# Constant loads on other queues, and the last turns of three stages inside the next job's fourth granule

## The reference

```python
# layer 1: sparse attention (NSA) and gated delta rule (GDN), merged by gates, then an MLP
h = rms_norm(x, ln1_w)
proj = h @ w_in
o_a = nsa_attention(nsa_q, nsa_kv, nsa_gate, rel_table, pe_k, pe_v, w1_k, w2_k, w1_v, w2_v)
o_b = gated_deltanet(gdn_qkv, gdn_z, gdn_a, gdn_b, conv_w, a_log, dt_bias, gdn_norm_w)
x = x + (g_a * (o_a @ w_pa) + g_b * (o_b @ w_pb)) @ w_o
h = rms_norm(x, ln2_w)
x = rms_norm(x + square(relu(h @ w_up)) @ w_down, ln_f_w)
# layer 2: attention with a forget gate (FOX)
y = (softmax_attention(q, k, v, forget) * silu(gate)) @ fox_w_out      # q, k, v, gate = x @ fox_w_in
x = layer_norm(ALPHA * x + y)
# layer 3: retention (RET)
y = (group_norm(retention(q, k, v)) * silu(gate)) @ ret_w_out          # q, k, v, gate = x @ ret_w_in
x = layer_norm(ALPHA * x + y)
```

## Time and profile before

| | us |
|---|---|
| three runs | 3129.84, 3130.97, 3135.68 (median 3130.97) |
| the profiled execution, from its first instruction to its last | 3131.4 |
| PE busy in it | 2893.7 (92%) |
| DVE busy | 1660.0 (53%) |
| ACT busy | 1297.6 (41%) |
| POOL busy | 54.6 (2%) |
| mean granted TensorE clock | 0.970 of full |

### The profile page before, as it was taken

The page is one execution under the profiler, slowest core; times in us unless marked ns, Lnnn a source line. Parts: engine busy times, 40 slices in busy tenths (PEclk is TensorE's granted clock), DMA queues, the critical chain, the costliest instruction groups (busy, mean ns, idle before and its releaser), DMA issues.

```text
span 3131.4 us, 36002 instructions
## 1 busy us (share of the span) xinstructions
PE 2893.7 (92%) x13617; PEld 2396.2 (77%) x13617; DVE 1660.0 (53%) x1879; ACT 1297.6 (41%) x1558; POOL 54.6 (2%) x57
## 2 busy tenths in 40 slices
PE   4998988899998999999999799999989999999997
PEld 3877777687777888888888677777767777877776
DVE  3554654744454555555555555555565455554555
ACT  3554633523434444444344444444334443443432
POOL 0000000000000000000000000000000000000000
PEclk9999999999999999999999999999989999999998
DMA  5753322314565556565655468568545554554553
GB/s 189 199 202 111 126 85 77 110 66 146 176 215 188 167 188 191 186 197 181 198 185 191 123 145 153 149 144 160 201 140 164 169 164 161 189 174 154 172 188 135
DMA packets 258376, 505.71 MB, mean 161 GB/s; under 512 B 12920, under 2 KB 22216, under 8 KB 256848
## 3 DMA queue, kind: packets, MB, share of 16 engines
q1 hardware_dynamic: 249552, 489.72, 51.1%
q0 software_dynamic: 2864, 13.32, 1.6%
q10 hardware_dynamic: 5840, 0.94, 0.2%
HBM read 500.26 MB, written 3.67 MB: 161 GB/s over the span
## 4 chain that ended last, share of the span: by engine, by line
PE 60%; issue 33%; DVE 3%; DMA 1%; ACT 1%; ACTq 1%; POOL 1%; DVEq 0%; POOLq 0%
PE acc L295 18%; PE acc L296 18%; PE acc L297 18%; PE mx L336 1%; DMA bias_by_distance<-arena 1%; PE acc L1423 1%; PE acc L1424 1%; PE acc L1425 1%; ACTq L800 1%; ACT w_hi L259 1%; PE mx L1559 0%; PE mx L1547 0%; ACT arena L383 0%; DMA arena<-bias_by_distance 0%; POOL sm L403 0%
## 5 line engine op out<-in xcount | busy, mean ns | idle before, releaser
L267 DVE TENSOR_TENSOR w_lo<-raw,w_hi 128x1024 fp32r<-128x1024 f32 x924 | 1133.1, 1227 | 1292.7 <-ACT w_hi L259 1279.9
L259 ACT ACTIVATE w_hi<-raw 128x1024 fp32r<-128x1024 f32 x924 | 978.7, 1060 | 1571.3 <-PE acc L297 1505.6
L295 PE MATMUL acc<-w_hi,lt_a_hi 128*128 128x512 f32 x2592 | 1040.4, 401 | 3.0 <-DVE w_lo L267 3.0
L296 PE MATMUL acc<-w_lo,lt_a_hi 128*128 128x512 f32 x2592 | 1018.3, 393 | 0.0
L297 PE MATMUL acc<-w_hi,lt_a_lo 128*128 128x512 f32 x2592 | 1017.8, 393 | 0.0
L295 PEld LDWEIGHTS acc<-w_hi,lt_a_hi 128*128 128x128 f32 x2592 | 494.2, 191 | 107.7 <-issue 7.2
L297 PEld LDWEIGHTS acc<-w_hi,lt_a_lo 128*128 128x128 f32 x2592 | 492.0, 190 | 105.2
L296 PEld LDWEIGHTS acc<-w_lo,lt_a_hi 128*128 128x128 f32 x2592 | 493.5, 190 | 102.0 <-issue 3.8
L295 PE MATMUL acc<-w_hi,lt_b_hi 128*128 128x512 f32 x896 | 351.0, 392 | 0.0
L297 PE MATMUL acc<-w_hi,lt_b_lo 128*128 128x512 f32 x896 | 349.8, 390 | 0.0
L296 PE MATMUL acc<-w_lo,lt_b_hi 128*128 128x512 f32 x896 | 349.8, 390 | 0.0
(11 more groups left out here) (313 smaller groups left out, 1719.7 us busy)
## 6 DMA issues: line engine op xcount, KB each, us to landing
raw<-in_ret_w_in SPq DMA_DIRECT2D x96, 1024.0 KB, 5.0
raw<-in_w_in SPq DMA_DIRECT2D x84, 1024.0 KB, 5.0
raw<-in_w_up SPq DMA_DIRECT2D x64, 1024.0 KB, 5.4
raw<-in_w_down SPq DMA_DIRECT2D x64, 1024.0 KB, 5.1
raw<-in_fox_w_in SPq DMA_DIRECT2D x64, 1024.0 KB, 7.3
raw<-in_ret_w_out SPq DMA_DIRECT2D x34, 1024.0 KB, 5.1
raw<-in_w_o SPq DMA_DIRECT2D x16, 1024.0 KB, 5.1
raw<-in_fox_w_out SPq DMA_DIRECT2D x16, 1024.0 KB, 5.1
```

Source lines behind the costliest of these rows:

```text
L259: nc.scalar.activation(w_hi[:, r % 4], raw[:, slot, 2 * half:2 * half + 2, :], ACT.Copy).then_inc(hi_ready, 1)
L267: nc.vector.tensor_tensor(w_lo[:, r % 4], raw[:, slot, 2 * half:2 * half + 2, :], w_hi[:, r % 4].bitcast(F32), ALU.subtract) \
L295: nc.tensor.matmul(o, a_hi, hi, start=(kt == 0), stop=False)
L296: nc.tensor.matmul(o, a_hi, lo, start=False, stop=False)
```

## The change

At the start, ACT's 15 loads go elsewhere. Five (one-hot, table, `conv_w` and two position tables; semaphore `prep_loaded`) are issued by SP behind job 0's four slots. The two of `wsmall` (semaphore `wsmall_loaded`) are issued by POOL ahead of the root, and the other eight (`const_loaded`) by POOL behind it. The waits follow: ACT's is for `wsmall` alone, PE's ahead of the preparing products is for the five of SP, and one wait for `const_loaded` is added on PE ahead of the product with `w2`.

In the three stages, the turn that stood on its own now stands in the next job's hook at granule 3. ACT and DVE run two splits of that job, the turn's copies, then the other six. DVE's product that the turn needs stands between those two splits. FOX's first job is taken out in front, so that the loop is `fori(3)` over the rest of a group and the next group's first job, with the last group written out behind it. RET's two pairs of a half and WO's four jobs are written out instead of looped.

```diff
-        N_CONST = 15
+        N_CONST = 8
@@ SyncE, behind load_job(sp, 0, ...)
+            for dst, src in ((onehot[0:BUCKETS, :], c_onehot), (tabl[0:BUCKETS, :], rel_table),
+                             (cw_nat[0:96, :], conv_w.rearrange("w (c p) -> (w c) p", p=P)),
+                             (pe_nat[0:CMP_BLOCK, 0, :], pe_k), (pe_nat[0:CMP_BLOCK, 1, :], pe_v)):
+                sp.dma_start(dst, src).then_inc(sg("prep_loaded"), 16)
@@ GpSimd
+            for dst, src in ((wsmall[:, :, 0:24], w_in[:, C_GATE:C_GDN].rearrange("(k p) n -> p k n", p=P)),
+                             (wsmall[:, :, 24:40], w_in[:, C_AB:C_MERGE].rearrange("(k p) n -> p k n", p=P))):
+                pool.dma_start(dst, src).then_inc(sg("wsmall_loaded"), 16)
             root_pool(pool, sg("ms_ready"), 1, ssum, rstd, NT, sg("rstd_ready"))
+            for dst, src in ((w2[:, 0, :, :], w2_k.rearrange("(c p) n -> p c n", p=P)),
...
+                pool.dma_start(dst, src).then_inc(sg("const_loaded"), 16)
@@ ScalarE
-            for dst, src in loads:
-                act.dma_start(dst, src).then_inc(sg("const_loaded"), 16)
             rms_act(act, 0)
             split_hi(act, 0, 0, 4)
             turn_hi(act, B_LN1, whole(lt_a), 8)
-            act.wait_ge(sg("const_loaded"), 16 * N_CONST)
+            act.wait_ge(sg("wsmall_loaded"), 16 * 2)
             few_hi(wsmall[:, :, :], 40)
...
+            split_hi(act, J_WO, 4, 6)
             turn_hi(act, B_Y + 6, part(lt_a, 12), 2)
+            split_hi(act, J_WO, 6, 12)
...
+            def fox_turn(J, g):
+
+                split_hi(act, J, 4, 6)
                 turn_hi(act, Lin(B_FO, [(2, g)]), part(lt_b, g * HG), 2)
+                split_hi(act, J, 6, 12)
...
+            def ret_turn(J, h, p):
+
+                split_hi(act, J, 4, 6)
+                turn_hi(act, Lin(B_RO + 2, [(8, h), (4, p)]), part(lt_b, p * 8 + 4), 2)
+                split_hi(act, J, 6, 12)
@@ TensorE
-            pe.wait_ge(sg("const_loaded"), 16 * N_CONST)
+            pe.wait_ge(sg("prep_loaded"), 16 * 5)
...
-            turn_y_block(3)
+            def last_y_block(r):
+
+                if r == 3:
+                    turn_y_block(3)
+
             pe.wait_ge(acc_taken[0], (J_WO + 1) // 2)
...
+            multiply(pe, J_WO, lt_a, J_WO % 2, last_y_block, fresh=B_Y)
...
-                wait(pe, sg("fo_ready"), Lin(1, [(1, g)]))
-                turn(pe, Lin(B_FO, [(2, g)]), lambda c, t: f_o[:, t, c, :], 2)
+            def fox_turn(g):
+
+                def hook(r):
+                    if r == 3:
+                        wait(pe, sg("fo_ready"), Lin(1, [(1, g)]))
+                        turn(pe, Lin(B_FO, [(2, g)]), lambda c, t: f_o[:, t, c, :], 2)
+                return hook
+
+            multiply(pe, J_FOX, lt_a, J_FOX % 2)
+            with fori(3) as g:
+                fox_group(g)
+                J = Lin(J_FOX + 4, [(4, g)])
+                multiply(pe, J, lt_a, J.c % 2, fox_turn(g))
+            fox_group(3)
+            multiply(pe, J_FOXO, lt_b, J_FOXO % 2, fox_turn(3), fresh=B_FO)
...
+            def ret_turn(h, p):
+
+                def hook(r):
+                    if r == 3:
+                        turn_y(h, p, 1)
+                return hook
@@ VectorE
             dve.wait_ge(sg("x_again"), 16)
+            split_lo(dve, J_WO, 4, 6)
+            turn_lo(dve, B_Y + 6, part(lt_a, 12), 2)
+            split_lo(dve, J_WO, 6, 12)
...
+            def fox_turn(J, g):
+
+                split_lo(dve, J, 4, 5)
                 wait(dve, acc_taken[0], Lin((J_FOX + 3) // 2 + 1, [(2, g)]))
                 fo = f_o[:, :, :, :].rearrange("p t h d -> p t (h d)")
                 TT(fo, fo, f_nat[:, 3], ALU.mult).then_inc(sg("fo_ready"), 1)
+                split_lo(dve, J, 5, 6)
                 turn_lo(dve, Lin(B_FO, [(2, g)]), part(lt_b, g * HG), 2)
+                split_lo(dve, J, 6, 12)
...
+            def ret_turn(J, h, p):
+
+                split_lo(dve, J, 4, 5)
+                gate_y(Lin(J_RET + 6 * p, [(16, h)]), Lin(p, [(2, h)]), 1)
+                split_lo(dve, J, 5, 6)
+                turn_lo(dve, Lin(B_RO + 2, [(8, h), (4, p)]), part(lt_b, p * 8 + 4), 2)
+                split_lo(dve, J, 6, 12)
```

More of the change, by code:

```diff
@@ L1084, in _ @@
                             mix = ret_mix(h, p)
+                        if p == 1 and c == 0:
+                            ret_turn(J, h, 0)
+                            take(act, J, J.c % 2, lambda t: A(r_nat[:, 0, t, :], acc[J.c % 2][t][:, :], ACT.Copy))
+                            continue
                         copy_job(J + c, lambda t, c=c: r_nat[:, c, t, :],
                                  ACT.Silu if c > 3 else ACT.Copy, RET_QK ** -0.5 if c == 1 else 1.0, mix=mix)
-                    turn_hi(act, Lin(B_RO + 2, [(8, h), (4, p)]), part(lt_b, p * 8 + 4), 2)
-                for c in range(4):
+                ret_turn(Lin(J_RET + 12, [(16, h)]), h, 1)
+                for c in range(1, 4):
                     split_hi(act, Lin(J_RET + 12 + c, [(16, h)]), 4, 12)
@@ L1565, in ret_mix @@
                 yield
+            def ret_turn(h, p):
[3 more added lines that the diff above has]
+                return hook
             with fori(2) as h:
-                with fori(2) as p:
-                    J = Lin(J_RET, [(16, h), (6, p)])
+                for p in range(2):
+                    J = Lin(J_RET + 6 * p, [(16, h)])
                     mix = None
@@ L1890, in _ @@
             dve.wait_ge(sg("x_again"), 16)
-            with fori(2) as i:
-                for c in range(2):
-                    J = Lin(J_WO + c, [(2, i)])
-                    splits(J)
-                    add_job(J, i * (2 * NB) + c * NB, "wo_done")
+            split_lo(dve, J_WO, 4, 6)
+            turn_lo(dve, B_Y + 6, part(lt_a, 12), 2)
+            split_lo(dve, J_WO, 6, 12)
+            for c in range(4):
+                if c:
+                    splits(J_WO + c)
+                add_job(J_WO + c, c * NB, "wo_done")
             rms_dve(dve, 1, h_nat)
@@ L1958, in fox_mix, with fox_group @@
                 yield from unit_dve(dve, Lin(4, [(1, g)]), fc, f_sc, f_o, f_bias[:, :, :], None, True)
[L1960 removed]
+            def fox_group(g):
                 fc = Chain(dve, sg("fox_dve_step"), Lin(0, [(K_FOX_DVE, g)]))
[L1962 to L1965 removed]
+                mix = fox_mix(g, fc)
+                for kind in range(1, 4):
                     splits(Lin(J_FOX + kind, [(4, g)]), mix)
+                fc.end(K_FOX_DVE)
+            def fox_turn(J, g):
+                split_lo(dve, J, 4, 5)
                 wait(dve, acc_taken[0], Lin((J_FOX + 3) // 2 + 1, [(2, g)]))
@@ L1969, in _ @@
                 TT(fo, fo, f_nat[:, 3], ALU.mult).then_inc(sg("fo_ready"), 1)
+                split_lo(dve, J, 5, 6)
                 turn_lo(dve, Lin(B_FO, [(2, g)]), part(lt_b, g * HG), 2)
-                fc.end(K_FOX_DVE)
+                split_lo(dve, J, 6, 12)
+            splits(J_FOX)
+            with fori(3) as g:
+                fox_group(g)
+                fox_turn(Lin(J_FOX + 4, [(4, g)]), g)
+            fox_group(3)
             def block_stats(c):
@@ L2097, in _ @@
                             mix = ret_mix(h, p, rc)
-                        splits(J + c, mix)
-                    gate_y(J, pr, 1)
-                    turn_lo(dve, Lin(B_RO + 2, [(8, h), (4, p)]), part(lt_b, p * 8 + 4), 2)
+                        if p == 1 and c == 0:
+                            ret_turn(J, h, 0)
+                        else:
+                            splits(J + c, mix)
                     rc.end(K_RET_DVE)
```

103 lines of the change are left out of this document (48 added, 55 removed).

## The result

The changed kernel takes **3079.85 us** (median of 4 runs, 3076.45 to 3081.67) against 3130.4 for the kernel before on the same chip. The ratio is 0.9829, with a 95% interval of 0.9815 to 0.9844. The forecast was 3061 with a range of 3054 to 3074, so the sign was right and the gain too large: 70 us forecast, 51 measured by the medians and 53.5 by the ratio. The profiled execution's span is 3080.0, against 3131.4.

What follows compares the result with a forecast made beforehand. PE was taken to set the pace, losing time at the start and nine standalone turns. Start 17.5, FOX 28.1, RET 23.7 and PAB to WO 0.9 sum to 70.2 us, taking 3131.4 to 3061, range 3054 to 3074.

Steps and rivals of the forecast that it cites:

- What bounds the kernel, the method: Whole kernel: PE sets the pace except at the start and nine standalone turns; MLP turns inside jobs cost 0.88 us.
- The start, 17.5: Start: moving ACT's loads brings the first matmul from 44.74 to 27.2 us, gaining 17.5; bounds 10.5 and 21.4.
- FOX, 28.1: Four FOX turns: 5.04 us of waiting saved at each, plus 7.9 of clock loss, sum 28.1 us.
- what is late next: FOX turn in the next job: DVE's product would end at 1876.2, 0.9 us ahead of PE reaching granule 3.
- FOX and RET in longer code have more or fewer loop turns and ends ... I count nothing for either: Small edits in FOX and RET: stalls are the same at a loop's turn and end, so no cost was counted.
- RET, 23.7: Four RET turns: 3.81 us of waiting saved at each, plus 8.5 of clock loss, sum 23.7 us.
- PAB to WO, 0.9: Between PAB and WO: PE still waits for the accumulator; gain 1.25 less 0.4, about 0.9 us.
- The cover of 1 to 2 us: WO's first job: DVE's first split, at 928.7, is ready 1 to 2 us before PE needs it.
- POOL takes ACT's place: Rival at the start: load issues hold POOL as they held ACT; start gives 10.5, total 3068 us; chance 0.14.
- The clock stays down: Rival in FOX and RET: clock losses of 7.9 and 8.5 remain, total 3077 us; chance 0.07.
- The moved turn is late: Rival in FOX and RET: product comes after PE reaches granule 3; 1 us at eight places, 3069; chance 0.10.

Runs made afterwards that it cites:

- with the load away: Changed kernel with ACT's FOX groups written out and a two-column Exp in each turn job, moving the table load there: 3079.42 us, one execution.
- The second and third execution of the changed kernel: The changed kernel, unedited, run again against the kernel before: 3077.95 us (ratio 0.9818), then 3078.51 us (ratio 0.982).

## Why the prediction was wrong, step by step

**What bounds the kernel, the method.** Right. Every wait named was where it was named. The MLP's price for a turn in a job held in FOX and RET: no idle PE at the turn, 22.65 us for a job with it against 21.76 without. In WO too PE did not wait at the turn.

**The start, 17.5.** The chain was right, its first term was not. The sum took the landings of the earlier trace rows as they stood, with slot 1 at 17.7, while the change put two loads of small pieces into the DMA engines by 5 us. The slot landed at 20.7, and that 3.0 is nearly all of the 3.1 missing: from the end of the two splits to the first matmul the forecast had 27.2 - 19.7 = 7.5, the trace has 7.64. The text looked for a harm of these loads on POOL's own time, and that rival fell: both issues end at 5.0, the root comes at 12.21. Its price was misread as well: of the 9.33 + 9.73 only the first row is a load of `wsmall`; the 9.73 is `in_cmp_w_k`, which the change puts behind the root. The sentence on the Trainium skill's page "DMA: Bandwidth & Descriptors", section "Issuing engines are not separate DMA queues", named the right mechanism, pieces that compete for the same engines wherever they are issued, but priced it as a wait of the root. What was not asked is the forecast's own question, who else waits for what the moved instruction uses.

**FOX, 28.1.** The term itself was right. From the jobs of kind 3 and 0 the four places gave 7.1, 6.5, 7.7 and 5.7, together 26.8, and the last would have been 6.7 but for a new step of 1.07 in front of its exponentials. What failed is the question "what is late next", which the text asked of the turn alone. It was answered with 0.9 of cover, and the trace has 1.17. The loss is one job further on: 1.56, 1.56 and 1.01 in kind 1's steps of groups 2 to 4, 1.07 in the last group's kind 2, 1.07 at its exponentials, and 1.3 and 1.6 of lower clock behind two of them, 9.2 in all. From 26.8 + 1.07 = 27.9 this leaves the 18.7 of jobs 65 to 79. (Three other traces of the moved turns give 17.1, 18.7 and 18.8 there. Job 64's step grew too, from 2.60 to 3.06; that is hidden, because the clock fell there in the kernel before and not in this trace of the changed kernel.) The sentence that failed is "FOX and RET in longer code have more or fewer loop turns and ends ... I count nothing for either". The loop's head carries ACT's table load, and the change moved the head from a job where nothing waits for ACT to one whose chain PE waits for. There it took 0.5 to 0.6, and the root came second, for another 0.93. The row that would have warned was in the trace of before: the first group's root with 2.73 instead of 1.64. What puts the root second is in part open. The load is not it alone: with the load away the root was still second, by 0.05 instead of 0.15, and in the last group, where no load stands in job 76 or ahead of the root in job 77, it is second by 0.12 and 0.05. What the traces show is that the root starts 0.25 us behind the start of the DVE instruction that releases it, and DVE's next split 0.10 to 0.20 behind it where it wins, 0.25 or more in the kernel before; what moved the split by that tenth in the last group, they don't show.

**RET, 23.7.** Right, 23.65. Its stage has no table load in the traces, and its roots take 0.69 and 0.71 as before. The second and third execution of the changed kernel give 23.9 and 24.0.

**PAB to WO, 0.9.** Right in kind. The wait is 3.60 (3.7 forecast); from job 23 to job 28 the gain was 0.4 in two traces of the changed kernel and 2.8 in the other, with the clock. The cover of 1 to 2 us held.

**The rest.** The forecast set jobs outside the change to zero, without a width. In the pair of traces that was compared two stretches of them cost 5.5 and 2.5 us; in the second execution of the changed kernel the lead at job 114 was 57.7, not 51.3, and in the third 53.8. The three ratios, 0.9829, 0.9818 and 0.982, lie within each other's intervals and stand for 53 to 57 us. Of 70 forecast, then, 3 went to the landings and 9 to FOX; the 1 to 5 that are left have the size of what the untouched jobs take from execution to execution, and whether the new start has a part in them is open.

**The rivals.** "POOL takes ACT's place" fell by the row of 2.52 us. "The clock stays down" fell where it was priced: 1.00 behind every moved turn of FOX and RET. It falls behind the small work's new, longer waits. "The moved turn is late" fell: covers of 1.17 and 1.8. Each was one step from what happened: the right resource with the wrong user, the right effect in the wrong job.

## What to carry to other kernels

When work moves, ask of each thing it uses (a queue, a table, a loop's head, a port) who else waits for that, not only whether the moved work is late. A loop whose boundary moves takes its table load along: put the boundary where that engine has slack. And where two engines start within a tenth of a microsecond of each other, a neighbouring edit can turn their order; a short harmless instruction turns it back, and here took 3.9 us of waits out of FOX.

## What the runs showed of the hardware

- A GpSimd power of 128x8 takes 1.64 us alone and 2.57 to 2.73 when a DVE subtraction of 128x1024 with both inputs in SBUF starts 0.15 to 0.05 before it, in one place 0.01 after it; it then ends 2.72 or 2.73 behind the subtraction's start. In the reverse order the subtraction takes 1.21 to 1.27. The order was the same in every execution of a kernel.
- 320 KB of small pieces issued at 2.5 to 5 us brought the DMA engines from 407 to 261 GB/s between 8 and 12 us at a busy share of 1.04 against 1.00, and the megabyte that the start waited for landed 4.5 us later.
- The same instructions, jobs 0 to 11, took 331.5 to 338.9 us in three executions of one kernel, with 15.8 to 34.1 us of them at 1.2 GHz. The total times of two profiles can't resolve less than that; the length of one wait, which was 3.06 or 3.07 in all three, can.
